# Two pairs of gate tiles computed in the projection stage instead of in the mixers, and four half tiles per chunk of the mixers instead of five

## The reference, cut to what matters

```python
proj = h @ w_in
(gq, gk, gv, g_low, gr, hq, hf, hi, hg, sz, sxbc, sdt, gates) = jnp.split(proj, offs, axis=-1)
...                                             # gates is 3 * 1024 columns wide
o = chunked_gated_linear_attention(q, k, v, log_a, GLA_CHUNK)        # GLA branch
o = chunked_gated_linear_attention(q, k, v, log_f, HGRN_CHUNK)       # HGRN branch
y = ssd_chunked_scan(xs, dt, a_neg, bm, cm, SSM_CHUNK)               # SSM branch
...
g = jax.nn.sigmoid(gates.astype(f32)).reshape(bsz, t_len, N_BRANCHES, D_MODEL).astype(dtype)
merged = (g[:, :, 0] * (y_gla @ w_br_gla)
          + g[:, :, 1] * (y_hgrn @ w_br_hgrn)
          + g[:, :, 2] * (y_ssm @ w_br_ssm))
return merged @ w_out
```

## Time and profile before

| | |
|---|---|
| runs | 2102.02, 2101.87, 2094.20 us |
| the profiled execution: its own time | 2096.52 us |
| its span, first to last instruction | 2094.8 us |
| PE busy, PEld busy | 1936.1 us (92%), 1585.3 us (76%) |
| DVE busy, ACT busy | 1481.2 us (71%), 1049.7 us (50%) |
| mean granted clock of PE | 0.967 of 2.4 GHz |
| projection, steps of seven products | 184 to 529 us |
| mixers | 579 to 1105 us, of which chunks 610 to 1085 us |

### The profile page before, as it was taken

How to read it: one execution, slowest core, us unless ns; L and a number is a source line. 1 busy time by engine, 2 the same in 40 slices (tenths; PEclk the granted TensorE clock), 3 DMA queues, 4 the chain that set the end, 5 groups by cost and what they waited for, 6 DMA issues and landing times. The chain is left out here.

```text
span 2094.8 us, 26906 instructions
## 1 busy us (share of the span) xinstructions
PE 1936.1 (92%) x10610; PEld 1585.3 (76%) x10611; DVE 1481.2 (71%) x1746; ACT 1049.7 (50%) x1235; POOL 212.0 (10%) x163
## 2 busy tenths in 40 slices
PE   6999999999999999899996998984899999999994
PEld 5789888888977767677775887873788888888872
DVE  5966476675257778788764565556799999999974
ACT  4234345444133545444444243322688888888863
POOL 2310000000110000000000000012122222222210
PEclk9999999999999999999998999996899999999997
DMA  5232234234164555566426644532899999999986
GB/s 164 83 141 90 93 101 141 88 105 131 61 176 136 165 152 153 143 164 167 126 84 266 228 185 158 232 129 96 330 376 383 393 387 385 391 388 383 388 317 250
DMA packets 212416, 436.12 MB, mean 208 GB/s; under 512 B 28018, under 2 KB 151042, under 8 KB 184770
## 3 DMA queue, kind: packets, MB, share of 16 engines
q1 hardware_dynamic: 180834, 361.97, 49.6%
q10 hardware_dynamic: 20576, 51.39, 7.0%
q0 software_dynamic: 10880, 21.03, 2.6%
HBM read 369.67 MB, written 81.43 MB: 215 GB/s over the span
## 5 line engine op out<-in xcount | busy, mean ns | idle before, releaser
L2718 DVE TENSOR_TENSOR gu_lo<-gate_raw,gu_hi 128x2048 fp32r<-128x2048 f32 x64 | 146.6, 2292 | 31.8 <-ACT gu_hi L2663 31.8
L1592 PE MATMUL psum<-h_hi,l_hi 128*128 128x512 f32 x384 | 160.1, 417 | 3.3 <-PEq L58 3.3
L1592 PE MATMUL psum<-h_lo,l_hi 128*128 128x512 f32 x384 | 161.6, 421 | 0.0
L1592 PE MATMUL psum<-h_hi,l_lo 128*128 128x512 f32 x384 | 158.2, 412 | 0.0
L2718 DVE TENSOR_TENSOR gu_lo<-up_raw,gu_hi 128x2048 fp32r<-128x2048 f32 x64 | 146.4, 2287 | 13.5 <-ACT gu_hi L2663 13.5
L2723 DVE TENSOR_TENSOR dn_lo<-dn_raw,dn_hi 128x2048 fp32r<-128x2048 f32 x62 | 142.0, 2292 | 16.3 <-ACT dn_hi L2673 13.0
L2673 ACT CAST dn_hi<-dn_raw 128x2048 fp32r<-128x2048 f32 x62 | 118.2, 1909 | 48.3 <-PE y_ps L2775 48.3
L2663 ACT CAST gu_hi<-up_raw 128x2048 fp32r<-128x2048 f32 x64 | 122.2, 1910 | 36.4 <-PE u_ps L2790 35.1
L2663 ACT CAST gu_hi<-gate_raw 128x2048 fp32r<-128x2048 f32 x64 | 122.3, 1912 | 32.5 <-PE g_ps L2790 32.5
L2431 PE MATMUL mpsum<-y_hi,wb_hi 128*128 128x512 f32 x256 | 104.4, 408 | 18.2 <-DVE y_lo L2186 13.6
L1248 ACT COPY l_out<-psum 128x512 f32<-128x512 f32 x48 | 28.1, 586 | 179.0 <-PE psum L1592 175.0
(11 more groups left out here) (439 smaller groups left out, 5222.5 us busy)
## 6 DMA issues: line engine op xcount, KB each, us to landing
gate_raw<-moe SPq DMA_DIRECT2D x66, 1024.0 KB, 8.4
up_raw<-moe SPq DMA_DIRECT2D x64, 1024.0 KB, 8.1
dn_raw<-moe SPq DMA_DIRECT2D x62, 1024.0 KB, 7.5
w_raw<-w_in SPq DMA_DIRECT2D x26, 1024.0 KB, 5.9
dn_raw<-w_br SPq DMA_DIRECT2D x15, 1024.0 KB, 6.8
l_raw<-w_gates ACTq DMA_DIRECT2D x24, 512.0 KB, 6.2
s_gates<-l_out ACTq DMA_DIRECT2D x48, 256.0 KB, 4.3
gate<-s_gates SPq DMA_DIRECT2D x16, 768.0 KB, 4.4
```

Source lines behind the costliest of these rows:

```text
L1592: ins = nc.tensor.matmul(psum[:, bank, :], w[t % 2][:, k, :], x[:, k, half * 512:half * 512 + 512], start=i == 0, stop=i == LATE_MM - 1, s ...
L2718: nc.vector.tensor_tensor(gu_lo[p][:], gu_raw[p][:], gu_hi[p][:].bitcast(F32), ALU.subtract).then_inc(gu_ready, 1)
```

## The change

Four of the 24 tiles of `gates` (`EARLY_T = 4`, two pairs) become two further steps of the projection. They are steps 0 and 1, ahead of the Silu steps, and use the same seven products. Their results are copied instead of passed through a Silu, and stored in the layout of the `gates` tensor. Their weights come by two transfers of 512 KB each from `w_gates` instead of one of 1 MB from `w_in`. The mixers keep 20 tiles, thus 40 half tiles: 5 before the first chunk, 4 in each, 3 behind the last. The 96 matmuls of filling in a chunk are spread over the same 15 places, 6 or 7 at each. On ACT and on DVE the calls of `late` are four per chunk and stand at other places.

```diff
-PROJECT_STORES = 20
+PROJECT_STORES = 22
+EARLY_T = 4
...
-    N = len(SILU) + len(CONV)
-    is_conv = lambda n: 3 <= n < N and n % 2 == 1
-    convs = lambda n: (n - 3) // 2
-    STEPS = [CONV[convs(n)] if is_conv(n) else SILU[n if n < 2 else n // 2 + 1] for n in range(N)]
+    GATES = EARLY_T // 2
+    N = GATES + len(SILU) + len(CONV)
+    is_conv = lambda n: 5 <= n < N and n % 2 == 1
+    is_gates = lambda n: 0 <= n < GATES
+    convs = lambda n: (n - 5) // 2
+    STEPS = [None] * GATES + [CONV[convs(n)] if is_conv(n) else SILU[n - GATES if n < 5 else n // 2] for n in range(GATES, N)]
...
+                if is_gates(n):
+                    for a in range(2):
+                        sp.dma_start(w_raw[:, t % 2, :, a * P:(a + 1) * P], io["w_gates"][2 * n + a].rearrange("p (k n) -> p k n", k=KT))\
+                            .then_inc(raw_loaded[t % 2], 16)
...
+                if is_gates(n):
+                    act.dma_start(dr["gates"][:, 2 * n + a, :, 0, :].rearrange("h p t -> p h t"),
+                                  row(n, a).rearrange("p (h t) -> p h t", h=2)).then_inc(stored[n % 2], 16)
...
-                    nc.scalar.activation(row(n, 0), row(n, 0), ACT.Silu).then_inc(out_ready, 1)
+                    nc.scalar.activation(row(n, 0), row(n, 0), ACT.Copy if is_gates(n) else ACT.Silu).then_inc(out_ready, 1)
...
-LATE_T = WIDTHS["gates"] // P
+LATE_T = WIDTHS["gates"] // P - EARLY_T
 LATE_H = 2 * LATE_T
-PREFIX, PER_CHUNK = 5, 5
+PREFIX, PER_CHUNK = 5, 4
...
@@ scalar, body(c)
                 relative(c, 2)
                 relative(c, 3)
-                late(h0)
                 if c:
                     ssm_squares(c - 1)
...
+                late(h0)
                 relative(c, 4)
                 act.wait_ge(small_ready, c + 1)
                 differences(range(SSM_HEADS // 2))
-                late(h0 + 1)
                 relative(c, 5)
...
                 differences(range(SSM_HEADS // 2, SSM_HEADS))
+                late(h0 + 1)
                 relative(c, 6)
-                late(h0 + 2)
...
-                late(h0 + 3)
+                late(h0 + 2)
...
-                late(h0 + 4)
+                late(h0 + 3)
...
@@ tensor
-            SLOT = LATE_MM // 3
+            SLOTS = 15
+            def slots(n=1):
+                for _ in range(n):
+                    i = place[0] % SLOTS
+                    place[0] += 1
+                    fill((i + 1) * PER_CHUNK * LATE_MM // SLOTS - i * PER_CHUNK * LATE_MM // SLOTS)
+            place = [0]
...
-                fill(SLOT)
+                slots()
```

More of the change, by code:

```diff
@@ L602, in _ @@
                     sp.wait_ge(prepared, t - 2)
-                sp.dma_start(w_raw[:, t % 2], io["w_in"][:, COLS[t][0]:COLS[t][0] + PAIR]
-                             .rearrange("(k p) n -> p k n", p=P)).then_inc(raw_loaded[t % 2], 16)
                 n = t - HEAD
+                if is_gates(n):
+                    for a in range(2):
+                        sp.dma_start(w_raw[:, t % 2, :, a * P:(a + 1) * P], io["w_gates"][2 * n + a].rearrange("p (k n) -> p k n", k=KT))\
+                            .then_inc(raw_loaded[t % 2], 16)
+                else:
+                    sp.dma_start(w_raw[:, t % 2], io["w_in"][:, COLS[t][0]:COLS[t][0] + PAIR]
+                                 .rearrange("(k p) n -> p k n", p=P)).then_inc(raw_loaded[t % 2], 16)
                 if is_conv(n):
@@ L614, in loaded @@
         def loaded(eng, t):
-            eng.wait_ge(raw_loaded[t % 2], 16 * ((t + 1) // 2))
+            eng.wait_ge(raw_loaded[t % 2], 16 * sum(2 if is_gates(u - HEAD) else 1 for u in range(t % 2, t + 1, 2) if u))
         @block.gpsimd
@@ L666, in send @@
                 act.wait_ge(out_ready, len(sent))
-                act.dma_start(STEPS[n][1][a * P:(a + 1) * P, :], row(n, a)).then_inc(stored[n % 2], 16)
+                if is_gates(n):
+                    act.dma_start(dr["gates"][:, 2 * n + a, :, 0, :].rearrange("h p t -> p h t"),
+                                  row(n, a).rearrange("p (h t) -> p h t", h=2)).then_inc(stored[n % 2], 16)
+                else:
+                    act.dma_start(STEPS[n][1][a * P:(a + 1) * P, :], row(n, a)).then_inc(stored[n % 2], 16)
             sent = []
@@ L716, in step @@
                 else:
-                    nc.scalar.activation(place(n, 1, 0), X[b], ACT.Silu).then_inc(x_read, 1)
+                    nc.scalar.activation(place(n, 1, 0), X[b], ACT.Copy if is_gates(n) else ACT.Silu).then_inc(x_read, 1)
                 upper(n + 1, 6)
@@ L722, in step @@
                 else:
-                    nc.scalar.activation(place(n, 1, 1), place(n, 1, 1), ACT.Silu).then_inc(out_ready, 1)
+                    nc.scalar.activation(place(n, 1, 1), place(n, 1, 1), ACT.Copy if is_gates(n) else ACT.Silu).then_inc(out_ready, 1)
                     act.wait_ge(x_read, n + 1)
@@ L1701, in body @@
                 ins.then_inc(xT_ready, 1)
-                fill(SLOT)
+                slots()
                 level(c, 5)
-                fill(SLOT)
+                slots()
                 level(c, 6)
-                fill(2 * SLOT)
+                slots(2)
                 pe.wait_ge(qk_ready, NE * c + NE)
```

10 lines of the change are left out of this document (5 added, 5 removed).

## The result

Four runs of the changed kernel have a median of 2143.22 us (2138.47 to 2149.26); the kernel before, with one more run, has 2100.64 (2094.20 to 2102.02). The ratio is 1.021, with a 95% interval of 1.0178 to 1.0242: slower by 43 us. The forecast was 2114, with a range of 2097 to 2124. In the mixers that means: 23.6 us were to be saved there, and 38.4 - 42.6, thus about 4 us, were lost.

The account below looks back on a forecast made before the run. PE was taken to bound the projection, the order of waits the mixers. +38.4 us less 23.6 saved (33.2 - 9.6) gave +14.8: 2111.3 or 2116.7 us by baseline, taken as 2114, range 2097 to 2124.

Parts of the forecast that it names:

- Term 1: Projection: two more steps of 84 matmuls cost 19.2 us each, all else hidden behind PE: +38.4 us.
- Step (a): Mixer chunk: the load of `wmat` keeps DVE's `wd` at +18.3 us; filling removed before it buys nothing.
- Step (b): Mixer chunk, ACT: moved eviction, store and rounding delay the exponential of level 4, and DVE's factors, by 2.0 us.
- Step (c): Mixer chunk: `cbm` starts at +23.8, PE reaches its transposes at about +22.0 and waits 2.5 instead of 1.4 us.
- (d): Mixer chunk, behind `cbm`: 12 filling matmuls instead of 16, 4.5 us instead of 5.4; level 6 factors at +33.7, before +33.2.
- (e): Mixer chunk's end: without a third eviction, k's transposes come at +39.0 instead of +41.5; chunk 56.1 us, 4.2 saved.
- Step (f): Mixers: PE's clock falls behind the 2.5 us wait at `cbm`, 1.6 us in six of eight chunks, 9.6 us lost.
- C: Rival, mixers: the chunk follows PE in full; net -6.7 us, 2092 to 2095 us; chance 0.13.
- D: Rival: projection steps cost over 19.2 us each, or a second moved call holds a chunk; +25 us, 2124; chance 0.10.
- its own signs: Mixers: forecast wrong if chunk takes 55 us or less, `cbm` wait is under 1.5 us, or clock stays 1.00 behind it.

Follow-up runs that it names:

- both edits: Changed kernel with filling split 6 at twelve places and 8 at three, and ACT's first eviction put back ahead of the squares: 2104.18 us, ratio 1.0029.
- the filling aligned: Changed kernel with filling split 6 at the first twelve places and 8 at the last three, so half tiles end with a place: 2113.50 us, ratio 1.0073.
- both edits and the layout: The kernel with both edits, and `b_ssm` stored in HBM by chunks so the `wmat` load reads contiguous 8 KB pieces: 2097.49 us, ratio 0.9991.
- the kernel before with the layout: Kernel before the change with only `b_ssm` stored in HBM by chunks, 8 x 16 x 128 instead of 16 x 1024: 2093.52 us, ratio 0.9971.

## Why the prediction was wrong

**Term 1** was right: +38.4 forecast, +39.2 measured alone. The terms that failed are those of the mixers: 23.6 us to be saved, about 4 us lost.

**Step (a)** was right about DVE, with a small error: `wd` starts at +17.5 in chunk 2 (forecast +18.3), 0.82 us behind DVE's own list. "The filling removed before that point buys nothing" holds.

**Step (b) is the step that failed.** It followed what the moved eviction does to the exponential behind it, 2.0 us, and not what it does to the one who waits for the eviction. The part that it did follow came out: DVE waits 2.63 us for the exponential of level 4 in chunk 2, where about 2.6 was forecast:

```profile
782.12 0.56 DVE L1469 TENSOR_TENSOR k_lv<-k_in,ex 128x384 f32<-128x384 f32 x1 [2.63 <-ACT ex L1273]
```

I named what is queued behind the moved eviction on ACT, but not who needs the bank that it frees. PE's `fill` waits for `l_evicted` at the first matmul of each half tile that shares a bank, and in the chunks all share bank 7. This wait was put at nothing, and it is 53.0 us in all, with the granted clock at 0.50 behind it. Of the 43 us, 36 go when the two edits take it away (42.6 - 6.5, each against the kernel before run beside it).

**Step (c)** had the wrong wait. PE does not come to the transposes behind `cbm` at +22.0 but at +28.5 in chunk 2 (788.82 - 760.29), held in the filling ahead of level 3, and its wait there is 1.0 us in total over all chunks instead of 2.5 in each. With both edits it is 1.7 us a chunk (13.8 / 8).

**Steps (d) and (e)** give 56.1 us for a chunk without the eviction's wait. With the filling aligned and ACT's moved order kept, which is the case they describe, 57.4 were measured, with 1.5 us a chunk still waited for the eviction. The saving in the mixers with both edits is 38.4 - 6.5 = 32 us (2104.18 against 2097.67), where 33.2 was forecast without the clock. That these numbers agree is in part luck. With the filling aligned the wait at `cbm` is 0.8 us in chunks 1 to 7 and not 2.5, and 30.3 us are waited at `q_lv`, 14.9 before, which no step foresaw. And the replay took chunk 2, which lasts 59.8 us, but its 56.1 was set against the mean of 60.3; against its own chunk it saves 3.7 us and not 4.2, 3 us less over six chunks.

**Step (f)**, the fall of the clock behind `cbm`, did not come there: the wait was gone. It came behind the eviction's wait, at 0.50 for 3.6 us, so the mechanism was right and its place wrong. The kernel with both edits tests it at its own place, as three of its waits for `cbm` are as long as forecast: behind 3.63 us (chunk 0) the granted clock was 0.57, behind 2.58 us (chunk 4) it was 0.53, and behind 2.51 us (chunk 5) it stayed at 1.00. Behind the other five, 0.5 to 1.4 us, it stayed at 1.00.

```profile
894.90:898.40 3.50, 3.50 (x12) 2.57 (x12) 3.47 (x4) 3.47 (x10) 0.00 (x0) 0.53 1.04 307
953.40:956.90 3.50, 3.50 (x37) 2.82 (x38) 3.47 (x4) 3.47 (x10) 0.00 (x0) 1.00 1.12 320
```

So "a wait of 2.5 us brings a fall in six chunks of eight" could not be had from the one example of chunk 4. The clock had also fallen in the kernel before behind waits at `q_lv` of 2.4 us (0.53 to 0.69 in chunks 1, 3, 5 and 7), which step (f) left out.

**Rivals.** C (PE decides, -6.7 us) was not reached by any run: the kernel with both edits and the layout is 4 us slower than the kernel before with the layout, and no version with the two steps beat its partner without them. D had the right sign and size in part (+25 us, 0.10 chance), "a chunk is held by a second moved call", with the wrong call named. By its own signs the forecast was wrong as well: the wait at `cbm` was under 1.5 us, and no fall of the clock followed it. The sign was right, but not for the reason given; the range ended 19 us too low, because every case in it was made of waits that were in the trace of before. The wait that decided had length zero there.

## What to carry to other kernels

When an eviction, a store or any release of a buffer is moved, ask first who waits for that buffer and what stands between the release and the next use, on both engines; a wait that the trace shows with zero length is still there, and its slack is the distance between the release and the next use (here the next use stood at 13 us of the chunk, and the release went from 11 to 21). When work is respread over places, count where its units end: a unit that ends inside a place puts its successor right behind it. And before moving matmuls out of a stage with idle time into one without, compare the price of what is added (here 38 us, certain) with the most that can be won (45 us, if every wait shrinks too).

## What the runs showed of the hardware that was not expected

The time of a broadcast load depended on how its source is cut: 1 MB to 128 partitions landed in 16.3 us from 16 pieces of 512 bytes per partition and in 6.3 us from one contiguous 8 KB piece (7.4 and 7.6 us in two other kernels), with the same destination. And 8 KB in 4-byte pieces took 12 to 13 us, and with it ahead on the same queue a 1 MB load took 27.4 us instead of 16.3; with so small a transfer the kernels were 45 and 56 us slower over eight chunks.

Waits of nearly the same length left the clock at 1.00 or were followed by about half of it: 2.51 and 2.58 us in the same execution. All seven waits of 4.0 us and more in the changed kernel's chunks were followed by 0.50.
